# Second SwiGLU feed-forward as 2 by 2 blocks in Strassen's scheme, with weight sums made by accumulating DMAs

## What is computed

```python
def _swiglu(x, w_gate, w_up, w_down):
    return (jax.nn.silu(x @ w_gate) * (x @ w_up)) @ w_down
...
h = h + 0.5 * _swiglu(_rms(h, p['g_ffn2']), p['w_ffn2_gate'], p['w_ffn2_up'], p['w_ffn2_down'])
return _rms(h, g_final)
```

## Time and profile before

| | us |
|---|---|
| median of 3 runs | 1363.66 |
| lowest, highest | 1362.72, 1368.11 |
| span of the profiled execution (first to last instruction) | 1364.6 |
| PE busy | 1327.9 |
| DVE, ACT, POOL busy | 620.6, 416.7, 337.0 |

### The profile page before, as it was taken

One profiled execution on the slowest core, in us unless ns is written; L12 is line 12 of the kernel. 1 busy time (PEld: TensorE's weight loads), 2 busy tenths in 40 slices (PEclk: granted clock), 3 DMA queues, 4 the chain that ended last, 5 costly groups with the idle time before them and its releaser, 6 DMA issues.

```text
span 1364.6 us, 28243 instructions
## 1 busy us (share of the span) xinstructions
PE 1327.9 (97%) x11640; PEld 1227.7 (90%) x11640; DVE 620.6 (45%) x1021; ACT 416.7 (31%) x694; POOL 337.0 (25%) x350
## 2 busy tenths in 40 slices
PE   7999999999999999989999999999999999999997
PEld 7999998999999998857777666999999999999997
DVE  5335336233437795534444555555433333333344
ACT  5232221222225221413333343343321222222234
POOL 0219237127313110622222220022120121021012
PEclk9999999999999999979999999999999999999998
DMA  6223212322215222449999998522222212322321
GB/s 240 85 70 108 89 58 71 108 73 82 93 46 195 74 76 73 134 172 340 331 338 337 331 320 314 200 99 87 84 71 98 94 66 88 108 70 85 104 67 66
DMA packets 78931, 189.12 MB, mean 139 GB/s; under 512 B 10226, under 2 KB 13203, under 8 KB 78515
## 3 DMA queue, kind: packets, MB, share of 16 engines
q1 hardware_dynamic: 73762, 176.90, 37.9%
q10 hardware_dynamic: 3024, 6.69, 1.3%
q0 software_dynamic: 2048, 4.20, 0.9%
HBM read 178.06 MB, written 9.69 MB: 138 GB/s over the span
## 4 chain that ended last, share of the span: by engine, by line
PE 81%; DVE 6%; DMA 4%; POOL 3%; ACT 2%; SPq 2%; issue 1%; another core or an unknown queue 1%; ACTq 0%; DVEq 0%; POOLq 0%
PE d L1718 61%; PE e L2008 6%; DMA kv<-kv_src 3%; DVE w_lo L1115 2%; PE e L2040 2%; SPq L401 1%; PE e L2059 1%; PE d L2072 1%; PE d L2093 1%; PE e L2043 1%; PE e L1738 1%; PE d L1738 1%; ACT w_hi L602 1%; PE e L1885 1%
## 5 line engine op out<-in xcount | busy, mean ns | idle before, releaser
L1115 DVE TENSOR_TENSOR w_lo<-raw,w_hi 128x1024 fp32r<-128x1024 f32 (+2 forms) x191 | 224.2, 1174 | 378.3 <-ACT w_hi L602 377.5
L1718 PE MATMUL d<-x_hi,w_hi 128*128 128x272 f32 x1616 | 337.6, 290 | 9.6 <-DVE w_lo L1325 6.8
L1718 PE MATMUL d<-x_hi,w_lo 128*128 128x272 f32 x1616 | 335.3, 289 | 0.0
L1718 PE MATMUL d<-x_lo,w_hi 128*128 128x272 f32 x1616 | 334.7, 289 | 0.0
L602 ACT CAST w_hi<-raw 128x1024 fp32r<-128x1024 f32 (+2 forms) x191 | 185.8, 973 | 466.8 <-PE d L1718 444.4
L1718 PEld LDWEIGHTS d<-x_hi,w_hi 128*128 128x128 f32 x1616 | 255.3, 189 | 12.1 <-DVE w_lo L1325 6.8
L1718 PEld LDWEIGHTS d<-x_lo,w_hi 128*128 128x128 f32 x1616 | 255.4, 190 | 0.0
L1718 PEld LDWEIGHTS d<-x_hi,w_lo 128*128 128x128 f32 x1616 | 253.6, 190 | 0.0
L966 POOL TENSOR_TENSOR hid<-silu,up 128x544 f32<-128x544 f32 x42 | 57.0, 1357 | 497.6 <-DVE up L1188 485.7
L1718 PE MATMUL d<-hid_hi,w_hi 128*128 128x272 f32 x640 | 134.5, 291 | 4.8 <-DVE w_lo L1115 2.7
L1718 PE MATMUL d<-hid_hi,w_lo 128*128 128x272 f32 x640 | 132.2, 288 | 0.0
(11 more groups left out here) (361 smaller groups left out, 1819.0 us busy)
## 6 DMA issues: line engine op xcount, KB each, us to landing
kv<-kv_src SPq DMA_DIRECT2D x256, 256.0 KB
raw<-w_gu SPq DMA_DIRECT2D x87, 512.0 KB, 3.4
raw<-w_post SPq DMA_DIRECT2D x34, 512.0 KB, 3.5
raw<-w_d1b SPq DMA_DIRECT2D x16, 384.0 KB, 3.2
raw<-w_d2b SPq DMA_DIRECT2D x16, 384.0 KB, 3.1
raw<-w_in SPq DMA_DIRECT2D x10, 512.0 KB, 3.4
gates<-gate_m ACTq DMA_DIRECT2D x12, 272.0 KB
raw<-w_d1a SPq DMA_DIRECT2D x8, 384.0 KB, 3.1
```

Source lines behind the costliest of these rows:

```text
L1115: nc.vector.tensor_tensor(w_lo[:, s % 2, 0:n, :], raw[:, raw_pos(s), 0:n, :], w_hi[:, s % 2, 0:n, :].bitcast(FP), ALU.subtract).then_inc(S ...
L1718: ins = mm(out[:, b, :], w[:, pos, c0 + k, :], x[:, k, b * HALF:(b + 1) * HALF], start=first, stop=stop)
```

## The change

**The scheme.** A product of a 2 by 2 matrix of weight blocks with a 2 by 2 matrix of activation blocks is made of 7 block products in place of 8 (Winograd's form, called P1 to P7 here), with sums of blocks ahead of it and sums of products behind. The two columns of activations are the two halves of the tokens, the two rows are two halves of the contraction.

- *Gate and up*, kind "g": rows are gate and up of one chunk, contraction 2 times 4 chunks. 20 of the 22 chunks are units of 7 products of 4 chunks; chunks 0 and 1 (`HEAD = 2`) stay 4 tiles of the old kind, which run while the sums of activations are made.
- *Down*, kind "d": rows are two output chunks, contraction 2 times 3 chunks of a block of 6. The first three blocks give 12 units of 7 products of 3 chunks. The last block of 4 stays as it was.
- A product is 12 (g) or 9 (d) matmuls of 272 columns, all in one PSUM bank. P6, P5, P3 and P4 accumulate on banks that P1 or P7 filled and that were read in between, so PE waits for those reads (`p1_out`, `p6_out`, `c22`).

**Activations.** The norm is applied before the products (`x_scaled`, 8 of 128x544), four sums of 128x1088 are made on DVE (`x_sum`), and seven operands of 128x1088 are split by ACT and DVE (`x7_split_hi`, `x7_split_lo`). POOL makes the sums of the hidden chunks of a pair (3 differences and a sum of 128x272, beside two products of 128x544), ACT and DVE split seven 272-column operands a pair.

**Weights.** Each product loads its own block, 256 KB (g) or 192 KB (d), in 11 slots (`wr`), split by ACT and DVE into 8 buffers (`ws_hi`, `ws_lo`); those for P1, P2 and P4 are blocks of the weights as given, and those for P5, P6, P7 and P3 are sums of blocks held in DRAM (`s2_a`, `s2_d`).

**Sums of weight blocks.** They are made during the first feed-forward and the mixer, in four groups (`GROUPS`): 8 g units, then three times 4 d and 4 g units. ACT issues plain copies from DRAM to DRAM, one or two after each of the 8 down tiles of each block of the first feed-forward: 12, 8, 8 and 8 copies, each of 2 or 4 units and one of four quantities. Then POOL issues accumulating DMAs (`accum_op`) on the copies in three dependent steps, 4 additions a unit: `weight_sums(0)` to `(5)` at the places below. POOL waits inside them for the copies and for earlier sums. SP waits for all (`sums3`) before the first weight of a product.

Core of the diff (marks of left out parts are lines of "..."):

```diff
+    GROUPS = ((("g", 0, 2), ("g", 2, 4), ("g", 4, 8)), (("d", 0, 4), ("g", 8, 12)), (("d", 4, 8), ("g", 12, 16)), (("d", 8, 12), ("g", 16, 20)))
+    QUARTER = {1: 2, 2: 0, 3: 0, 4: 1}
+    ADDED = {1: 3, 3: 2}
+
+    def weight_block(kind, x, i0, i1):
+        row, half = divmod(x, 2)
+        if kind == "g":
+            t0, t1 = SUMMED[i0], SUMMED[i1 - 1] + 1
+            return a["w_gu2"][2 * t0 + row:2 * t1 + row - 1:2, :, half * KC // 2 * P:(half + 1) * KC // 2 * P]
...
@@ ACT, down tiles of each block of the first feed-forward
                 for m in range(KC):
                     split_hi(s + m + 2, t + m + 1)
+                    weight_copies(b, m)
...
+        def weight_copies(g, m):
+            copies = [(kind, q, i0, i1) for kind, i0, i1 in GROUPS[g] for q in (1, 3, 2, 4)]
+            for kind, q, i0, i1 in copies[m * len(copies) // KC:(m + 1) * len(copies) // KC]:
+                nc.scalar.dma_start(summed(kind, q, i0, i1), weight_block(kind, QUARTER[q], i0, i1)).then_inc(sem["cp%d" % g], 16)
...
@@ POOL
                     input_weights()
+                    weight_sums(0)
...
                     output_weights()
+                    weight_sums(1)
...
+                    add_squares(N_MIX, KC)
+                    weight_sums(2)
...
+        def long_rows(ap):
+            return ap.rearrange("u p n -> (u p n)").rearrange("(r n) -> r n", n=2048 if ap.shape[2] == KC // 2 * P else 1536)
+
+        def weight_sums(step):
+            if 0 <= step - 2 < len(GROUPS):
+                pool.wait_ge(S.sums2, 16 * sum(len(g) for g in GROUPS[:step - 1]))
+                for kind, i0, i1 in GROUPS[step - 2]:
+                    pool.dma_start(long_rows(summed(kind, 4, i0, i1)), long_rows(summed(kind, 2, i0, i1)), accum_op=ALU.add,
+                                   max_dma_last_dim=8192).then_inc(S.sums3, 16)
+            if 0 <= step - 1 < len(GROUPS):
+                pool.wait_ge(S.sums1, 32 * sum(len(g) for g in GROUPS[:step]))
+                for kind, i0, i1 in GROUPS[step - 1]:
+                    pool.dma_start(long_rows(summed(kind, 2, i0, i1)), long_rows(summed(kind, 1, i0, i1)), accum_op=ALU.add,
+                                   max_dma_last_dim=8192).then_inc(S.sums2, 16)
+            if step < len(GROUPS):
+                pool.wait_ge(sem["cp%d" % step], 64 * len(GROUPS[step]))
+                for kind, i0, i1 in GROUPS[step]:
+                    for q, x in ADDED.items():
+                        pool.dma_start(summed(kind, q, i0, i1), weight_block(kind, x, i0, i1), accum_op=ALU.add,
+                                       max_dma_last_dim=8192).then_inc(S.sums1, 16)
...
         nc.gpsimd.memset(hprev[:, :, :, :, 0:1], 0.0).then_inc(S.hprev_zero, 1)
         add_squares(N_Q, QC)
+        weight_sums(3)
         pool.wait_ge(S.evac, S_MIX + MIX.index("r") + 1)
         nc.gpsimd.tensor_tensor(ktrig[:, :], kraw[:, :], trig[:, :], ALU.mult).then_inc(S.ktrig_done, 1)
         add_squares(N_KV, LC)
+        weight_sums(4)
...
         pool.wait_ge(S.q_done, H)
+        weight_sums(5)
...
@@ DVE, ahead of the products
+            split_lo(s + 2, n=8)
+            inverse(N_FFN2, rstd)
+            evacuate(0)
+            split_lo(s + 3, n=8)
+            for c in range(KC):
+                x_scaled(c)
+                if c == KC - 2:
+                    evacuate(1)
+            x_sum(x_t1[:, :, :], xn[:, 1, :, :], xn[:, 3, :, :], ALU.subtract, 1)
+            x_sum(xn[:, 1, :, :], xn[:, 0, :, :], xn[:, 1, :, :], ALU.subtract, 2)
+            x7_split_lo(0)
+            x7_split_lo(1)
+            part_lo(0)
+            part_lo(1)
+            evacuate(2)
+            x_sum(xn[:, 0, :, :], x_t1[:, :, :], xn[:, 0, :, :], ALU.subtract, 3)
+            x7_split_lo(2)
+            part_lo(2)
+            x7_split_lo(3)
+            part_lo(3)
+            x7_split_lo(4)
+            part_lo(4)
+            x_sum(xn[:, 2, :, :], xn[:, 2, :, :], xn[:, 0, :, :], ALU.add, 4)
+            evacuate(3)
...
+            for k, (typ, n) in enumerate(ORDER):
+                dve.wait_ge(*after("pr", k + 1))
+                product_out(typ, n)
+                part_lo(k + NWS)
...
@@ PE, last block: first(m) has three of the four chunks of down tile m
+            pe.wait_ge(*after("h7l", 2 * NQ + nb - 1))
+            first(0)
+            product(NP - 2)
+            product(NP - 1)
+            for m in range(1, KC):
+                first(m)
```

More of the change, by code:

```diff
@@ L98, in build @@
     BGLU = DSKIP + UC
+    s5p_at = cursor[0]
     s5p = new("s5p", [16, ST])
@@ new lines, in build @@
+    SUMMED = [t for t in range(sum(BLOCKS)) if t not in [tile_of(j) for j in range(HEAD)]]
+    assert SUMMED == [1, 2] + list(range(4, 22)) and BLOCKS == (6, 6, 6, 4)
+    DB = KC // 2
+    GROUPS = ((("g", 0, 2), ("g", 2, 4), ("g", 4, 8)), (("d", 0, 4), ("g", 8, 12)), (("d", 4, 8), ("g", 12, 16)), (("d", 8, 12), ("g", 16, 20)))
[5 more added lines that the diff above has]
+            t0, t1 = SUMMED[i0], SUMMED[i1 - 1] + 1
+            assert t1 - t0 == i1 - i0
+            return a["w_gu2"][2 * t0 + row:2 * t1 + row - 1:2, :, half * KC // 2 * P:(half + 1) * KC // 2 * P]
+        b, i = divmod(i0, DB)
+        w = BLOCKS[0] // 2 * P
+        src, c = (a["w_d2a"], half * w) if b == 0 else (a["w_d2b"], (2 * (b - 1) + half) * w)
+        i1 -= b * DB
+        return src[2 * i + row:2 * i1 + row - 1:2, :, c:c + w]
@@ new lines, in before_unit, with bank, hidden_ready @@
+    def before_unit(n, kind):
+        return sum(1 for m in range(n) if UNITS2[m][0] == kind)
+    def bank(n, x):
+        i = 3 * (n % 2) + x
+        return e[:, i, 0:HALF] if i < 3 else d[:, (i - 3) // 2, (i - 3) % 2, 0:HALF]
+    def hidden_ready(q):
+        n = UNIT_OF["g", 2 * q + 1] if 2 * q + 1 >= HEAD else -1
+        b = next(b for b in range(NB) if q < sum(BLOCKS[:b + 1]) // 2)
+        if b and q == sum(BLOCKS[:b]) // 2:
+            return AT["P4", UNIT_OF["d", (b - 1, KC // 2 - 1)]]
+        return AT["P3", n + 1]
@@ L270, in build @@
+    NQ = (sum(BLOCKS) - NLAST) // 2
+    READY = {hidden_ready(q): q for q in range(NQ)}
+    assert len(READY) == NQ and len(set(BLOCKS[:-1])) == 1
+    L_FREE = AT["P4", UNIT_OF["d", (NB - 2, KC // 2 - 1)]]
+    L_THIRD = AT["P5", NU - 1]
     W_IN = {"r": 0, "v0": 1, "v1": 2, "c0": 3, "c1": 4, "c2": 5, "u0": 6, "u1": 7, "u2": 8, "u3": 9}
@@ L585, in _ @@
             post(s)
-        ffn_slots(S_FFN2, 2, 0)
+        for i in range(2 * HEAD):
+            slot(S_FFN2 + i, a["w_gu2"][2 * tile_of(i // 2) + i % 2], 8)
+        sp.wait_ge(S.sums3, 16 * sum(len(g) for g in GROUPS))
+        for k in range(NP + KC):
+            if 3 <= k < NWR:
+                sp.wait_ge(S.lo_done, S_FFN2 + (k - 3) // 2 + 1)
+            if k >= NWR:
+                sp.wait_ge(*after("w_lod", k - NWR + 1))
+            if k >= NP:
+                src, n = a["w_d2b"][k - NP, :, (BLOCKS[1] + BLOCKS[2]) * P:], NLAST
+            else:
+                typ, u_ = ORDER[k]
+                src, n = unit_source(u_, typ), steps(u_)
+            sp.dma_start(wr[k % NWR][:, 0:n, :], src.rearrange("p (c n) -> p c n", n=P)).then_inc(sem[WR_IN[k % NWR][0]], 16)
         for x in range(2):
@@ L667, in gate_up @@
                     for r in range(4):
[L668 to L673, removed]
+                        if r != 1 or not first:
+                            split_hi(s + r + 2, t + r + 1 + 4 * i, i, nb if last and r >= 2 else 8)
                         if r == 0 and first:
```

513 lines of the change are left out of this document (407 added, 106 removed).

## The result

| | before | after |
|---|---|---|
| median, us (4 runs each) | 1365.9 | 1634.7 |
| lowest, highest | 1362.7, 1368.4 | 1627.1, 1642.0 |
| span of the profiled execution | 1364.6 | 1636.8 |
| ratio of the times, 95% interval | | 1.197 (1.192 to 1.202) |

The forecast was 1338, faster than before, with a range of 1326 to 1500: the kernel became slower, and its time lies outside the range.

What follows compares the result with a forecast made beforehand. The second feed-forward was taken as bound by PE's number of matmuls: 43.5 saved - 8 - 2.2 - 1 - 1 - 5 = 26.3 us, giving 1338 us, with a range of 1326 to 1500.

Steps and rivals of the forecast that it cites:

- 348 matmuls at 125 ns, 43.5 us: Second feed-forward: 2820 matmuls in place of 3168, at an unchanged 125 ns each, save 43.5 us.
- Changes from g to d, 1 us: Second feed-forward, three changes from g to d units: the last pair's splits cost 1 us in all, bounds 0 and 15.
- Weights from DRAM: Second feed-forward: loading 256 KB per product in 1.5 us needs 175 GB/s against 346 reached, so free.
- Start, 8 us (4 to 14): Start of the second feed-forward: PE waits for DVE's work on sums and operands, 8 us lost, bounds 4 and 14.
- End, 2.2 us (0 to 4): End of the second feed-forward: PE waits for the third hidden chunk, 2.2 us lost, bounds 0 and 4.
- 36 issues on ACT of about 0.33 us ... 1 us, bounds 0 and 5: First feed-forward: ACT's issuing of the copies costs 1 us, showing only in block 3.
- ACT or SP held at an issue: A listed sign that the forecast is wrong: one of these engines standing while it issues a DMA.
- For a copy I take the loads' 346 GB/s with ... a quarter off: DRAM copies in the first feed-forward: 260 GB/s, so 32 us for group 0 and 28 for each other group.
- few-engines rival: Copies run on only as many DMA engines as they have units, delaying POOL's step 3 and PE: 1472 us, chance 0.30.
- point from which it decides: Test for copies on a few engines: it holds as soon as the copies of group 3 end after 503.
- POOL's issues, 7.5 to 11 us a step: First feed-forward and mixer: POOL's 36 accumulating DMA issues take 5 to 11 us a step, covered by gaps.
- Late sums, 5 us: Mixer: step 4's additions finish issuing late and delay the query sums, 5 us lost; `ktrig` not late.

Runs made afterwards that it cites:

- e5: The changed kernel with its copies but no accumulating DMAs (sums left out, for timing only); 1501.0 us.
- e1: The changed kernel with the 128 rows as outermost dimension in copies and first sums; 1349.7 us, ratio to before 0.9963.
- e9: e1 with copies and additions dealt out one or two at a time, and the second feed-forward's start reordered; 1344.2 us, ratio to before 0.9846.
- e7: e1 with all copies in the down tiles of blocks 0 to 2 and additions at nine places; 1365.1 us, ratio to before 1.0014.

## Why the prediction was wrong, by its steps

- **348 matmuls at 125 ns, 43.5 us:** right (11640 to 11292; 2312 matmuls in 290 us).
- **Changes from g to d, 1 us:** 0. **Weights from DRAM:** free, as forecast: no wait of PE for `wr`.
- **Start, 8 us (4 to 14): 19.** In the first 56.5 us 283 matmuls, against 436 in the same stretch before: 153 x 0.125 = 19.1. PE stood 15.6 us (before 1.2), and the granted clock was 0.91 in place of 1.00, another 5 us, a term that the sum didn't have. The list of DVE's work was right (P1 starts 19.3 us behind the start of DVE's reciprocal, 18.4 forecast); what was left out is that PE also waits for ACT's and DVE's read-outs, which stand behind that work in their queues.
- **End, 2.2 us (0 to 4):** one wait of 2.6 us for `lh_lo`; the last 47 us have 273 matmuls, before 305 in 46.6, so 4.4 us with the clock.
- The two stretches in the kernel before, for the comparison of these two steps:

```profile
950.30:1006.80 56.50, 55.30 (x436) 54.72 (x435) 21.74 (x20) 19.24 (x22) 11.09 (x9) 1.00 0.24 79
...
1318.00:1364.60 46.60, 38.58 (x305) 38.20 (x303) 23.16 (x53) 22.26 (x47) 12.09 (x14) 0.92 0.24 76
```

- So the second feed-forward gained 43.5 - 19.1 - 4.4 = 20.0, measured 21.0, forecast 32.3.
- **"36 issues on ACT of about 0.33 us ... 1 us, bounds 0 and 5": this step failed.** It took an issue's price from a DMA that found its queue empty. An issue took 11.0 us in the median, and the copies alone made the kernel 165 us later (e5). The bounds were of an issue's own work, and left out that the engine stands at an issue until earlier copies have gone on. "ACT or SP held at an issue" was listed among the signs of being wrong, but no sum had a price for it.
- **"For a copy I take the loads' 346 GB/s with ... a quarter off": failed by the shape.** The few-engines rival had the price (12.1 us for a g copy; 11 measured) but led it only through POOL's steps and `ktrig`, with ACT free: 1472. The true path was ACT's queue, already in block 0, at 93 us. Its "point from which it decides" (copies ending after 503) was therefore wrong too. At 0.30 it should have been the largest case, since nothing spoke against it but that no such spread was in the trace.
- **POOL's issues, 7.5 to 11 us a step:** right where the rows are outermost (7.5 us for the first six in e1); with units outermost POOL was held up to 59 us.
- **Late sums, 5 us:** 15.8 in e1. `ktrig` was 6.3 us late (forecast 0), but the greater part is a mechanism that the sum had not: loads of weights that land late beside the sums (ACT waited 13.9, 5.4 and 9.3 us for three). Behind `ktrig` it isn't POOL that is late: its query sums wait for DVE. The rate was right: two steps, 15 MB, kept DMA full from 430 to 530, 150 GB/s beside the loads (forecast 130).
- With the shape mended, the forecast's 1338 against 1363.7 (0.981) compares with 0.9963 as the change places its sums, and 0.9846 (e9, the fastest against its own chip's time) when they are dealt out.

## What to carry to other kernels

Look at the slowest dimension of a DMA from DRAM to DRAM before its bytes: 2 or 4 in front of 128 rows made 0.5 or 1 MB take 11 us and held the engine that issued it, on a queue where PE's weights stood behind. Never cost an issue by the price that a nearly empty queue shows; ask what is queued behind the issuing engine if it stands. Bulk transfers beside a tight stream of loads are dealt out one or two at a time: the same 60 MB, all but 4 of them ahead of the cache pages, cost 16 us up to there in bursts and 4 dealt out.

## What the runs showed of the hardware that was not expected

- ACT's queue took two few-engine copies (1.2 and 2.9 us) and then gave way only as fast as one drained (some 11 us), whether it had 0.5 or 1 MB. Copies with the rows outermost went in 0.56 us, but in e7, where they landed after some 40 us, they held ACT for 12.1 and 7.9 us too. What fills the queue wasn't tried.
- POOL is held at an issue likewise, 59.1 us at the longest, and a reshaped sum leaves it in fewer packets: the software queue had 41344 packets for 34.8 MB in the changed kernel, 12672 for 34.6 MB in e1. What splits them wasn't tried.
- An accumulating DMA of 1 MB with 128 long rows landed after 20.1 us in the median in bursts (e1) and 14.2 dealt out (e9); copies of that size after 9.9 and 11.9.
- On top of its idle time PE pays for holes by the clock: in 90 to 210 us the granted clock was 0.73, a mean between its two levels of 1.2 and 2.4 GHz, with PE busy 56 of 120 us; in 1300 to 1590, with no hole, it was 1.00.
